# Group 0's recurrence in a streaming encoder layer: where its exponentials, level operands and level scores stand in the queues

## What is computed

```python
def hgrn2_chunk(s0, q, k, v, logf):
    cum = jnp.cumsum(logf, axis=2)
    decay = jnp.exp(jnp.where(causal[..., None], cum[:, :, :, None, :] - cum[:, :, None, :, :], -jnp.inf))
    attn = jnp.einsum('bhtk,bhsk,bhtsk->bhts', q, k, decay)
    o = jnp.einsum('bhtk,bhkv->bhtv', q * jnp.exp(cum), s0) + jnp.einsum('bhts,bhsv->bhtv', attn, v)
    last = cum[:, :, -1:, :]
    s_new = jnp.exp(last[:, :, 0, :])[..., None] * s0 + jnp.einsum('bhsk,bhsv->bhkv', k * jnp.exp(last - cum), v)
    return s_new, o
```

## Time and profile before

| | before |
|---|---|
| median of 3 runs (lowest to highest) | 3797.7 us (3796.08 to 3798.84) |
| profiled execution: time, span | 3802.48 us, 3800.7 us |
| busy: PE, DVE, POOL, ACT | 3110.5 (82%), 2685.5 (71%), 2233.9 (59%), 873.0 us (23%) |
| moved by DMA, mean rate | 1409.65 MB, 371 GB/s |
| share of the row fetches' queue (q0) in 16 DMA engines | 78.0% |
| mean granted clock of PE | 0.924 of 2.4 GHz |

### The profile page before, as it was taken

One profiled execution on the slowest core, in us unless ns is written; L12 is line 12 of the kernel. 1 busy time (PEld: TensorE's weight loads), 2 busy tenths in 40 slices (PEclk: granted clock), 3 DMA queues, 4 the chain that ended last, 5 costly groups with the idle time before them and its releaser, 6 DMA issues.

```text
span 3800.7 us, 35321 instructions
## 1 busy us (share of the span) xinstructions
PE 3110.5 (82%) x11076; PEld 1832.4 (48%) x11076; DVE 2685.5 (71%) x5855; ACT 873.0 (23%) x2072; POOL 2233.9 (59%) x2224
## 2 busy tenths in 40 slices
PE   5787988897788999897799998986888898875555
PEld 4565755553356545552467455532565455321112
DVE  0335668679967696699686786799685764897775
ACT  2112222122222221222241221222231312221101
POOL 0012444576766575666665675667674754777775
PEclk8887899999899999999989999998999999998768
DMA  6478888999999999999999999999999999999998
GB/s 183 155 261 279 290 304 299 382 404 397 383 393 400 398 406 404 408 406 371 396 389 396 393 407 404 407 398 377 396 397 401 410 401 369 396 410 409 410 409 337
DMA packets 443263, 1409.65 MB, mean 371 GB/s; under 512 B 46528, under 2 KB 48064, under 8 KB 442312
## 3 DMA queue, kind: packets, MB, share of 16 engines
q0 software_dynamic: 316960, 1152.82, 78.0%
q1 hardware_dynamic: 101520, 201.08, 14.5%
q10 hardware_dynamic: 24600, 53.51, 4.0%
HBM read 1389.91 MB, written 19.95 MB: 371 GB/s over the span
## 4 chain that ended last, share of the span: by engine, by line
PE 36%; DMA 22%; DVE 18%; POOL 12%; issue 9%; ACT 2%; ACTq 0%; DVEq 0%; POOLq 0%
PE PS L668 16%; POOL ring L648 11%; DMA ring<-in_peer_v,idx 11%; PE PS L975 9%; DMA wring<-in_w_in 7%; DVE ring L1734 6%; PE PS L672 5%; DMA ring<-in_peer_u,idx 2%; PE PS L865 1%; PE PS L762 1%; PE PS L787 1%; DVE arena L1436 1%; DVE arena L1441 1%; DMA wring<-in_peer_query 1%; DVE acc L1745 1%
## 5 line engine op out<-in xcount | busy, mean ns | idle before, releaser
L975 PE MATMUL PS<-ring,diag 128*128 128x512 f32 (+1 forms) x3032 | 1550.9, 645 | 426.2 <-DMA ring<-in_peer_v,idx 394.5
L1734 DVE CUSTOM_DVE_ANT_0 ring<-ring,PS 128x1024 f32<-128x1024 f32 x1088 | 1311.9, 1212 | 274.7 <-DMA ring<-in_peer_u,idx 266.5
L648 POOL DMA_INDIRECT ring<-in_peer_u,idx x1088 | 1103.5, 1014 | 680.1 <-PE PS L975 306.2
L648 POOL DMA_INDIRECT ring<-in_peer_v,idx x1088 | 1110.0, 1020 | 620.5 <-DVE hid L1734 330.0
L975 PEld LDWEIGHTS PS<-ring,diag 128*128 128x128 f32 (+1 forms) x3032 | 556.9, 198 | 1212.6 <-issue 949.6
L668 PE MATMUL PS<-xnT,wring 128*128 128x256 f32 (+2 forms) x3840 | 768.0, 359 | 58.8 <-DMA wring<-in_w_in 39.4
L668 PEld LDWEIGHTS PS<-xnT,wring 128*128 128x128 f32 x3840 | 677.0, 199 | 177.9 <-issue 49.4
L1745 DVE SCALAR_TENSOR_TENSOR acc<-ring,wk,acc 128x1024 f32<-128x1024 f32 x330 | 424.5, 1286 | 67.6 <-issue 39.5
L1341 ACT ACTIVATE diag<-masks,wk 128x128 f32<-128x128 f32 x704 | 260.7, 396 | 675.0 <-PE PS L975 524.9
L672 PE MATMUL PS<-wring,xnT 128*128 128x512 f32 (+1 forms) x432 | 191.7, 596 | 10.0 <-DMA wring<-in_w_in 9.8
L1532 DVE SCALAR_TENSOR_TENSOR arena<-PS,arena 128x256 f32<-128x256 f32 (+4 forms) x72 | 47.8, 664 | 144.9 <-PE PS L762 94.2
(11 more groups left out here) (218 smaller groups left out, 2485.4 us busy)
## 6 DMA issues: line engine op xcount, KB each, us to landing
wring<-in_w_in SPq DMA_DIRECT2D x110, 1024.0 KB, 11.9
wring<-in_peer_query SPq DMA_DIRECT2D x40, 1024.0 KB, 12.1
wring<-in_w_out SPq DMA_DIRECT2D x20, 1024.0 KB, 11.7
ring<-in_peer_u,idx POOLq DMA_INDIRECT x1088, 13.7
ring<-in_peer_v,idx POOLq DMA_INDIRECT x1088, 13.9
arena<-rel_scr ACTq DMA_DIRECT2D x80, 144.0 KB, 6.3
wring<-in_w_branch_a SPq DMA_DIRECT2D x10, 1024.0 KB, 16.4
wring<-in_w_branch_b SPq DMA_DIRECT2D x10, 1024.0 KB, 14.5
```

What stands on the lines that cost most here:

```text
L648: pool.indirect_dma_start(ring[:, SLOT[n], :], None, u_tab if kind == "u" else v_tab, bass.IndirectOffsetOnAxis(ap=idx[:, at:at + 1], axis ...
L975: mm = pe.matmul(PS[0:rows, 6 + half, :], diag[:, seq % ND, 0:rows], ring[:, SLOT[n], 512 * half:512 * (half + 1)], start=(seq == pe_of[tn ...
L1734: dve.tensor_tensor_reduce(row, row, xp_row, 1.0, 0.0, ALU.mult, ALU.add, hid[:, m % 2, k:k + 1]).then_inc(dve_used, 1)
```

## The change

The change touches group 0 alone, but for one semaphore. For group 0:

- ACT takes the exponentials (`decays`) in stage E, ahead of its wait for product "i"; DVE makes the level differences for them right behind the scans, and behind the exponentials `decayed` and the level operands of head 0, all before the multiply of T2.
- The level operands of odd heads go into a second pair of buffers, `L2`, in two slots of `ring`; DVE makes those of head h + 1 before it multiplies head h's scores.
- PE issues head h's level scores ahead of the outputs of head h - 1, and for that waits itself that the products of stage E have left PSUM.

For all groups the scores of the next head wait for the mask multiply (`hg_am`) in place of the sum over levels (`hg_red`); for DVE `hg_am` stands for the link between multiply and sum. The other groups' order stays.

```diff
+        L2 = cut(ring[:, HELD:HELD + 2, :].rearrange("p a b -> p (a b)")[:, 0:2 * NL * P], 2, NL, P)
...
+        hg_am = sem("hg_am")
...
+                    if g == 0:
+                        for n in set_ends[g, "E"][-2:]:
+                            pe.wait_ge(*freed(n))
+                    yield
+
+                    def level_scores(h):
+                        fh = ft * HB + h
+                        pe.wait_ge(hg_L, fh + 1)
+                        if fh >= 1:
+                            pe.wait_ge(hg_am, fh)
+                        lq, lk = (L2[:, 0], L2[:, 1]) if g == 0 and h % 2 else (Lq, Lk)
+                        for lev in range(NL):
+                            pe.matmul(PS[0:rows, lev // 4, (lev % 4) * P:(lev % 4) * P + rows],
+                                      lk[:, lev, 0:rows], lq[:, lev, 0:rows], start=True, stop=True)
...
                     for h in range(HB):
                         fh = ft * HB + h
+                        if g == 0:
+                            level_scores(h)
                         if h >= 1:
                             outputs(h - 1)
                         turn_keys(h)
                         yield
 
-                        pe.wait_ge(hg_L, fh + 1)
-                        if fh >= 1:
-                            pe.wait_ge(hg_red, fh)
-                        for lev in range(NL):
...
+                        if g > 0:
+                            level_scores(h)
                         pe.wait_ge(hg_kdc, fh + 1)
...
+                def decays(ti):
+                    tid, rows, c0 = tiles[ti]
+                    ft = tile_no[g, ti]
+                    act.wait_ge(hg_D, ft + 1)
+                    view = E[:, :, :, :].rearrange("p l h t -> p (l h) t")[:, :, 0:rows]
+                    act.activation(view, view, ACT.Exp)
+                    act.activation(ecum[:, :, 0:rows], Q[:, :, c0:c0 + rows], ACT.Exp).then_inc(hg_E, 1)
...
                     _, _, _, kind, what, c, ti = products[n]
+                    if g == 0 and what == "i":
+                        decays(0)
                     act.wait_ge(pj_ready, n + 1)
...
+                def level_operands(ti, h):
+                    tid, rows, c0 = tiles[ti]
+                    fh = tile_no[g, ti] * HB + h
+                    if g > 0:
+                        dve.wait_ge(hg_at, fh)
+                    elif h >= 2:
+                        dve.wait_ge(hg_at, fh - 1)
+                    lq, lk = (L2[:, 0], L2[:, 1]) if g == 0 and h % 2 else (Lq, Lk)
...
                         for h in range(HB):
-                            dve.tensor_tensor_scan(Q[:, h, 0:W], restart[:, 0:W], Q[:, h, 0:W], 0.0, ALU.mult, ALU.add)
+                            i = dve.tensor_tensor_scan(Q[:, h, 0:W], restart[:, 0:W], Q[:, h, 0:W], 0.0, ALU.mult, ALU.add)
+                        if g == 0:
+                            link(i)
+                            for _ in level_differences(0):
+                                pass
+                            dve.wait_ge(*freed(en[3]))
+                            decayed(0)
+                            level_operands(0, 0)
...
                     for h in range(HB):
                         fh = ft * HB + h
-                        if fh >= 1:
-                            dve.wait_ge(hg_at, fh)
...
+                        if g > 0:
+                            level_operands(ti, h)
+                        elif h + 1 < HB:
+                            level_operands(ti, h + 1)
                         yield
                         yield
                         dve.wait_ge(hg_at, fh + 1)
...
-                        i = dve.tensor_tensor(Am[0:rows, :, 0:rows], at, masks[0:rows, :, 0:rows], ALU.mult)
-                        yield
-                        link(i)
+                        dve.tensor_tensor(Am[0:rows, :, 0:rows], at, masks[0:rows, :, 0:rows], ALU.mult)\
+                           .then_inc(hg_am, 1)
+                        yield
+                        dve.wait_ge(hg_am, fh + 1)
```

More of the change, by code:

```diff
@@ L826, in mix @@
                         pe.wait_ge(state_loaded, 16)
+                    if g == 0:
+                        for n in set_ends[g, "E"][-2:]:
+                            pe.wait_ge(*freed(n))
                     yield
+                    def level_scores(h):
[7 more added lines that the diff above has]
+                                      lk[:, lev, 0:rows], lq[:, lev, 0:rows], start=True, stop=True)
+                        pe.matmul(PS[0:rows, 1, 2 * P:2 * P + rows], K2[:, h, c0:c0 + rows],
+                                  Q2[:, h, c0:c0 + rows], start=True, stop=True).then_inc(hg_at, 1)
                     def turn_keys(h):
@@ L1211, in mix @@
                     yield
[L1212 to L1215, removed]
+                    if g > 0:
+                        decays(ti)
                     yield
@@ L1563, in mix, with level_differences @@
                 yield from gated(g, "D", W)
[L1565 to L1577, removed]
-                            dve.tensor_tensor_scan(Q[:, h, 0:W], restart[:, 0:W], Q[:, h, 0:W], 0.0, ALU.mult, ALU.add)
-                    yield
[L1580 to L1585, removed]
-                link(i)
[L1588 to L1592, removed]
+                def level_differences(ti):
+                    tid, rows, c0 = tiles[ti]
                     ft = tile_no[g, ti]
@@ L1617, in mix @@
                        .then_inc(hg_kq, 1)
+                def level_operands(ti, h):
+                    tid, rows, c0 = tiles[ti]
+                    fh = tile_no[g, ti] * HB + h
[4 more added lines that the diff above has]
+                    lq, lk = (L2[:, 0], L2[:, 1]) if g == 0 and h % 2 else (Lq, Lk)
+                    dve.tensor_tensor(lq[:, :, 0:rows], E[:, 0:NL, h, 0:rows],
+                                      Q2[:, h:h + 1, c0:c0 + rows].to_broadcast([P, NL, rows]), ALU.mult)
+                    dve.tensor_tensor(lk[:, :, 0:rows], E[:, 0:NL, h, 0:rows],
+                                      K2[:, h:h + 1, c0:c0 + rows].to_broadcast([P, NL, rows]), ALU.mult)\
+                       .then_inc(hg_L, 1)
@@ new lines, in mix @@
+                en = by_stage[g, "E"]
+                for i_ in range(len(parts[g, "E"])):
+                    if 6 <= i_ <= HB + 5:
+                        h = i_ - 6
+                        dve.wait_ge(*freed(en[h // 2]))
+                        i = dve.tensor_scalar(K2[:, h, 0:W], Q[:, h, 0:W], one_lb[:, h:h + 1], lb[:, h:h + 1],
+                                              ALU.mult, ALU.add)
+                        if h == HB - 1:
+                            i.then_inc(f_fg, 1)
+                    if i_ == 13:
+                        dve.wait_ge(f_ln, g + 1)
+                        link(dve.tensor_scalar(K2[:, :, 0:W], K2[:, :, 0:W], -1.0, 1.0, ALU.mult, ALU.add))
+                        for h in range(HB):
+                            i = dve.tensor_tensor_scan(Q[:, h, 0:W], restart[:, 0:W], Q[:, h, 0:W], 0.0, ALU.mult, ALU.add)
[7 more added lines that the diff above has]
+                    yield
@@ new lines, in mix @@
+                for n in set_ends[g, "E"][-2:]:
+                    dve.wait_ge(*freed(n))
+                dve.wait_ge(gh_in, 16 * (g + 1))
+                for ti, (tid, rows, c0) in enumerate(tiles):
+                    i = dve.tensor_tensor(T2[0:rows, ti, :], T2[0:rows, ti, :], gain_hgrn[0:rows, :], ALU.mult)
+                yield
+                link(i)
+                if g == 0:
+                    dve.wait_ge(consts, 22)
+                if g == SG:
+                    dve.wait_ge(state_loaded, 16)
@@ L1618, in mix @@
+                for ti, (tid, rows, c0) in enumerate(tiles):
+                    ft = tile_no[g, ti]
+                    nch = rows // CH
+                    if g > 0:
+                        yield from level_differences(ti)
+                    else:
+                        yield
+                        yield
+                    yield
+                    yield
+                    if g > 0:
+                        decayed(ti)
                     yield
```

18 lines of the change are left out of this document (5 added, 13 removed).

## The result

The changed kernel takes 3773.94 us, median of 4 runs (3771.76 to 3775.62), against 3798.27 for the kernel before beside it. The ratio is 0.9932, with a 95% interval of 0.992 to 0.9943: 24 us less, between 22 and 30. The forecast was 3772.0, the range 3767 to 3781.

What follows compares the result with a forecast made beforehand. Group 0's uncovered chain of waits ahead of the first fetch, then full DMA engines, was taken as the bound; 13.4 (front) plus 12.3 (turns) made 25.7 off the median 3797.7, giving 3772.0 us, range 3767 to 3781.

Steps and rivals of the forecast that it cites:

- The lead-in: Group 0's stretch between stage E and the transposes ending at 196.09, ahead of the fetches; 25.7 us was to come off.
- The front: Group 0 up to head 0's mask multiply: differences, exponentials and operands moved into DVE's idle time; 13.4 us gained.
- The cover: PE's projections of "i" and "g" hide the moved work, costed at nothing; head 0's operands have 8.4 us to spare.
- The turns: Head 0's to head 3's mask multiply in group 0, DVE and PE no longer taking turns; 12.3 us gained.
- The 5.08 a head: DVE's time per head in group 0 if it never waits: 3.34 plus 1.74 for operands; DVE sets the pace.
- The tail: Group 0 from head 3's mask multiply to the transposes on PE, left as it was at 8.74 us.
- The clock: PE in group 0's recurrence taken at full clock, after group 1's row with 1.00 at 3.47 of 5 us busy.
- half clock: Rival: PE at half clock in group 0's recurrence, 6.5 us a head, gain 21.4, 3776.3 us; chance 0.20.
- The total: Whole kernel: 25.7 us gained, 13.4 in the front and 12.3 in the turns; 3772.0 us against the median.

Runs made afterwards that it cites:

- the delay: The changed kernel with 24 linked memsets of 128x1024 on DVE between group 0's last head and the root (also called the delayed kernel): 3802.39 us.
- the front alone: The changed kernel with one pair of operand buffers, operands after the last head's state update, and PE's outputs ahead of scores: 3786.59 us, ratio 0.9967.
- the old order on PE: The changed kernel, both buffer pairs kept, with PE's outputs of the last head and turned keys ahead of the scores: 3783.93 us, ratio 0.9958.

## Why the prediction was right

- **What bounds.** The lead-in stood on the path, and what came off it came off the end: shown by the delay, by the column of gains, and by the stretch from the first fetch to the end, which kept its length. No run changes the semaphore alone, but group 1's heads kept their pace with it.
- **The front.** Costed at 13.4; it went from 15.89 to 2.48, 13.41. The cover held: head 0's operands were done at 136.07 (135.12 + 0.95), 7.88 ahead of T2's multiply where I had 8.4 ahead of the scores. The copy of "i" still waited for PE, and the new table load lay in a gap of ACT.
- **The turns.** Costed at 12.3; 25.76 became 13.61, 12.15. The 5.08 a head is 5.11 and 5.12.
- **The tail.** Left as it was at 8.74; it took 8.43.
- **The clock.** I took full clock from one row of group 1 and named half clock as the rival at 3776.3. The rows showed full clock, in two of three executions for all four heads and in the third for three. That this term came out is in part luck. The row was no guide: PE had eight matmuls of the retrieval between those heads, and the next head's scores there, in the same trace of before, took 2.93:

```profile
556.08 3.70 PE L975 MATMUL PS<-ring,diag 128*128 128x512 f32 x8
...
562.74 2.93 PE L865 MATMUL PS<-arena 128*128 128x128 f32 x12 [0.63 <-DVE arena L1625]
```

  My reading that a warm start decides was too simple as well: the front alone also starts warm and loses the clock in the first head. What helped is that the fall of a single head costs the changed order little, at most 0.9 us in these executions.
- **The clock rule of the Trainium skill** (TensorE: Matmul & The Clock Gate, Part 1), that activity releases the throttle and idling restores it, gave the sum at full clock, and the change's rows agree with it, 1.00 from 148 to 160. For a PE that is busy part of the time the rows went both ways: after a window with 2.54 of 4 us busy the clock stayed at 1.00 in the change, after one with 2.53 it fell to 0.58 in the delayed kernel, and in neither had PE stood idle for more than 0.93 us at a time since the first scores.
- **The total.** 25.7 was forecast and 24.3 measured, with the interval on both sides of it; the lead-in gave 25.9. The further 1.8 us by which the changed profile starts T2's multiply earlier belongs to no term: over the profiles with the change's stage E that multiply starts anywhere from 143.45 to 146.72, so it is drift of the stages before.

## What to carry over

Work that waits at the head of a stage only because it is written there can go into the idle time of the stage before, if its operands already stand; the price is read from what else is in those queues. Where two engines take turns, put the next item's operands and products ahead of the last item's results, and check that the shorter of the two then fits inside the longer. An order that leaves an engine waiting can cost twice on PE, once as the wait and once in the clock behind it; matmuls that do nothing, put into the gap, tell the two apart.

## What I had not expected

- The old order of PE's queue costs 5.2 us of lead-in by itself and 4.8 through the clock.
- PE at full clock for the first head is no sign for the second: scores of 1.50 were followed by 2.42 with the front alone and by 2.47 with the old order on PE, after waits for DVE of 3.28 and 3.74 us.
- In the change's own recurrence one head's scores fell in two of four executions, after no such wait; with one operand buffer two heads' scores fell in both. What decides this stays open.
